# Rotary page columns: one wide transpose and one block-diagonal product for four pages

## The chip, the cores and the metric

One Trainium2 chip, one of its cores. The metric is the device time of one execution in microseconds (us); the number given for a kernel is the median of its timed runs.

## The reference, cut to what matters

One inference step of a hybrid decoder layer, for 1,024 prompt tokens and 64 sample tokens (8 requests of 8 tokens) with the same weights: a combined projection, a pooling mixer, latent attention with 8 heads, a gated merge, and a retrieval of experts. The change lies in the attention of the sample tokens over the paged cache, 32 pages of 128 positions for each request:

```python
def mla_keys(c, kr, p):
    k_nope = jnp.einsum('btc,chd->bthd', c, p['w_uk'])
    kr_b = jnp.broadcast_to(kr[:, :, None, :], k_nope.shape[:-1] + (QK_ROPE,))
    return rmsnorm(jnp.concatenate([k_nope, kr_b], axis=-1), p['k_norm_w'])

def page_step(carry, phys):
    m, l, acc = carry
    c_pg = ckv_pages[phys]
    k_pg = mla_keys(c_pg, kr_pages[phys], p)
    s = jnp.einsum('bqhd,bthd->bhqt', q, k_pg).astype(jnp.float32) * SCALE
    return online_update(m, l, acc, s, c_pg), None
```

A page has 256 latent columns (c) and 32 rotary columns (kr) for each of 128 positions. A score is the product of a query with c in latent form, plus the product of its 32 rotary numbers with kr, times one over the key's norm. The expert part (`peer`) gathers, for each token, 128 rows of 4 KB from `peer_u` and 128 from `peer_v`, and dots and weighs them.

## The kernel before, in words

Everything is fp32. **Experts** is the main program. It is cut into slots: for one slot the four compute engines and SyncE do what belongs to one expert column of 128 tokens. GpSimd issues one indirect gather of 128 rows of `peer_u` and, 20 slots later in the numbering, one of `peer_v` (L1550); VectorE makes a dot product of 1,024 columns (L1658) and, spread over 16 slots, the search for the best experts of a later unit (L1417 to L1488) ; TensorE adds the weighted `peer_v` rows in blocks of 8 products, one block for every 4 slots (L1613). Rings of 8 buffers hold the gathered rows. There are 1,088 such columns.

All other work is laid into these slots by hand: `Main.to(slot)` (L180) issues the main program up to a slot and then lets the caller add its own instructions. Instructions of an engine run in the order in which they are written; semaphores join the engines.

**Pages** (L1730) is the sample attention over the cache. It works in 64 groups (8 requests of 8 groups) of 4 pages; the last group of a request has a fifth page, the request's own new tokens. A group takes 6 slots. For page j of a group:

- `transposes` (L1834) turns the page on TensorE into PSUM (`tp`): two transposes of 128x128 for the latent columns (L1840), one of 128x32 for the rotary ones (L1841).
- `copy_page` (L1917) on ScalarE copies them to SBUF into `cTp[j % 2]`: 128x256 (L1922), then 32x128 (L1923), then a drain.
- `keys` (L1843) on TensorE makes the page's keys, two products of 512 columns (L1850), and then the scores, two products of 64 columns over the latent rows (L1858) and one over 32 rotary rows (L1859). It waits for the square of the page before, since all pages use one PSUM bank for keys.
- `square` (L1930) on ScalarE squares the keys out of PSUM, and `key_norm` (L1990) on VectorE sums the squares per head.

TensorE writes the transposes of page j + 1 ahead of the keys of page j (L1903 to L1908). After the last page of a group ScalarE and VectorE make norms, scaled scores and the maximum over the pages (L1936, L1996, L1941, L2010, L2017); TensorE turns the maxima (`maxima`, L1863) in the first slot of the next group, behind the first transposes of that group and ahead of the others; VectorE makes the new maximum, TensorE spreads it (`spread_maxima`, L1868, behind the keys of page 1), VectorE subtracts (L2033), ScalarE takes exponentials (L1945, L1950, in slot 3), and TensorE weighs the pages (`weigh`, L1875, behind the keys of the last page).

SyncE loads the page table, `w_uk` and the queries before the first group (`load_first`, L1780): latent queries `qlat`, and the rotary queries `qrope`, 32 rows by 512 columns for all requests. It then loads pages by groups, three groups of buffers (L1800), and each request's new rows (L1792). GpSimd clears the buffers that need it (`clear`, L1817).

## Time and profile before

| | |
|---|---|
| median of 3 timed runs | 4246.88 us (4240.99 to 4273.01) |
| the profiled execution, its time | 4212.48 us |
| its span, first to last instruction | 4210.3 us |
| TensorE busy | 3178.9 us (76%) |
| VectorE busy | 2688.5 us (64%) |
| GpSimd busy | 2417.2 us (57%) |
| ScalarE busy | 972.6 us (23%) |
| mean granted TensorE clock | 0.852 of full speed |
| moved by DMA | 1387.22 MB, mean 329 GB/s |
| the pages' stretch (L1840 to L1859) | from 1965.5 to 3412.6 us of the span |

The engines appear as PE (TensorE's matmuls), PEld (its weight loads), DVE (VectorE), ACT (ScalarE), POOL (GpSimd) and SP (SyncE). A row of the timeline has the start, the duration, the engine, the line, what is written and read, and how many records were joined; an fp32 product or weight load of the kernel leaves two records. Ends of matmuls are modelled, so the distance from one start to the next says more than the durations. The time outside the span is 2.2 us.

### The profile page before, as it was taken

What the parts mean: (1) busy time and instruction counts of PE and PEld (TensorE: products, weight loads), DVE (VectorE), ACT (ScalarE), POOL (GpSimd) and SP (SyncE); (2) the same over time, 40 slices, a digit from 0 to 9 for tenths busy, and PEclk for the clock granted to TensorE, in tenths of its full rate; (3) what the DMA queues carried; (4) which work ended last, traced back from release to release, by engine and by line L of the source; (5) the groups of instructions that cost most, each with busy time, mean ns of one, the idle gap of its engine ahead of it and who ended that gap; (6) DMA issues with size and microseconds to landing.
All of it is one profiled execution on the core that took longest, in us unless ns stands there. A gap on an engine that the chain in (4) does not pass through costs nothing.

```text
span 4210.3 us, 46249 instructions
## 1 busy us (share of the span) xinstructions
PE 3178.9 (76%) x13875; PEld 1687.6 (40%) x13875; DVE 2688.5 (64%) x6876; ACT 972.6 (23%) x2083; POOL 2417.2 (57%) x2194
## 2 busy tenths in 40 slices
PE   8896867987796889785888888798887866553335
PEld 5665424533342544342444444444444434230001
DVE  2313976665677766665777777787877765566543
ACT  1200222111122210200444334443353311100000
POOL 0000545665675566666666666666656666577766
PEclk9698978998997889897999999998999977666578
DMA  4445887999999899999888999898989899899999
GB/s 120 100 155 180 312 314 283 411 396 384 384 408 319 285 373 411 397 411 374 320 322 318 329 334 323 306 340 317 331 302 329 321 355 414 330 407 375 364 382 346
DMA packets 431352, 1387.22 MB, mean 329 GB/s; under 512 B 59033, under 2 KB 117370, under 8 KB 426818
## 3 DMA queue, kind: packets, MB, share of 16 engines
q0 software_dynamic: 313344, 1140.99, 71.6%
q1 hardware_dynamic: 117762, 243.29, 16.6%
q8 instruction: 113, 1.85, 0.2%
q14 instruction: 133, 1.09, 0.1%
HBM read 1353.98 MB, written 30.11 MB: 329 GB/s over the span
## 4 chain that ended last, share of the span: by engine, by line
PE 41%; POOL 14%; DVE 12%; DMA 12%; issue 11%; another core or an unknown queue 3%; ACT 2%; DVEq 2%; SPq 1%; ACTq 0%; POOLq 0%
POOL arena L1550 14%; PE ps L1850 10%; PE ps L1613 7%; DMA arena<-in_peer_v,arena 6%; DVE arena L1658 4%; PE ps L915 3%; PE ps L972 2%; PE ps L705 2%; PE ps L1858 2%; DMA arena<-in_peer_u,arena 2%; PE ps L1840 2%; DMA arena<-in_w_peer 2%; PE ps L1859 2%; PE ps L937 2%
## 5 line engine op out<-in xcount | busy, mean ns | idle before, releaser
L1550 POOL DMA_INDIRECT arena<-in_peer_v,arena x1088 | 1185.4, 1090 | 1000.8 <-PE ps L1613 660.5
L1658 DVE CUSTOM_DVE_ANT_0 arena<-arena 128x1024 f32<-128x1024 f32 x1088 | 1321.4, 1222 | 564.2 <-DMA arena<-in_peer_u,arena 457.3
L1550 POOL DMA_INDIRECT arena<-in_peer_u,arena x1088 | 1230.7, 1131 | 766.4 <-DVEq L1488 396.6
L1613 PE MATMUL ps<-arena 128*32 128x512 f32 x4352 | 702.3, 733 | 466.0 <-DMA arena<-in_peer_v,arena 418.7
L1850 PE MATMUL ps<-arena 128*128 128x512 f32 x1056 | 557.5, 653 | 17.8 <-ACT arena L1930 10.1
L1613 PEld LDWEIGHTS ps<-arena 128*32 128x32 f32 x4352 | 146.1, 124 | 865.8 <-issue 852.7
L1990 DVE TENSOR_REDUCE arena<-arena 128x8 f32<-128x512 f32 x264 | 180.7, 685 | 221.1 <-ACT arena L1930 186.2
L972 PE MATMUL ps<-arena 128*128 128x384 f32 (+1 forms) x768 | 249.3, 478 | 57.9 <-DMA arena<-in_w_peer 56.1
L1850 PEld LDWEIGHTS ps<-arena 128*128 128x128 f32 x1056 | 198.7, 209 | 199.8 <-issue 185.3
L1930 ACT ACTIVATE arena<-ps 128x512 f32<-128x512 f32 x264 | 157.7, 597 | 358.2 <-PE ps L1850 291.0
L915 PE MATMUL ps<-arena 128*128 128x384 f32 (+1 forms) x768 | 233.9, 460 | 2.1 <-ACT arena L1129 2.1
L1858 PEld LDWEIGHTS ps<-arena 128*128 128x128 f32 x1056 | 166.7, 199 | 141.0 <-issue 141.0
L972 PEld LDWEIGHTS ps<-arena 128*128 128x128 f32 x768 | 150.3, 202 | 146.2 <-issue 80.1
L1922 ACT ACTIVATE arena<-ps 128x256 f32<-128x256 f32 x264 | 101.4, 384 | 455.0 <-PE ps L1841 261.3
L705 PE MATMUL ps<-arena 128*128 128x384 f32 (+1 forms) x528 | 172.0, 485 | 18.1 <-DVE arena L1201 16.6
L915 PEld LDWEIGHTS ps<-arena 128*128 128x128 f32 x768 | 147.5, 194 | 89.0 <-issue 16.5
L1863 PE MATMUL ps<-const,arena 128*64 128x128 f32 x64 | 22.5, 352 | 173.6 <-DVE arena L2017 97.3
L1858 PE MATMUL ps<-arena 128*128 128x64 f32 x1056 | 151.4, 267 | 0.0
L1627 ACT ACTIVATE arena<-arena 32x1024 f32<-32x1024 f32 x120 | 126.4, 1053 | 90.4 <-DVE arena L1658 69.7
L705 PEld LDWEIGHTS ps<-arena 128*128 128x128 f32 x528 | 102.9, 197 | 88.3 <-issue 28.9
L1840 PE MATMUL ps<-const,arena 128*128 128x128 f32 x528 | 121.7, 315 | 19.8 <-ACTq L1924 13.8
L1875 PE MATMUL ps<-arena 128*64 128x257 f32 x528 | 129.5, 389 | 5.2 <-ACT arena L1950 5.2
(226 smaller groups left out, 4013.0 us busy)
## 6 DMA issues: line engine op xcount, KB each, us to landing
arena<-in_w_merge SPq DMA_DIRECT2D x32, 1536.0 KB
arena<-in_w_peer SPq DMA_DIRECT2D x64, 576.0 KB
arena<-in_cache SPq DMA_DIRECT2D x256, 144.0 KB
arena<-in_peer_u,arena POOLq DMA_INDIRECT x1088
arena<-in_peer_v,arena POOLq DMA_INDIRECT x1088
arena<-in_w_front SPq DMA_DIRECT2D x33, 512.0 KB
arena<-in_w_out SPq DMA_DIRECT2D x24, 512.0 KB
arena<-s_dram SPq DMA_DIRECT2D x68, 128.0 KB
```

The lines of the kernel that those rows point to most:

```text
L705: last = t.matmul(bank, w[:, k, :], xnT[:, k, :], start=k == 0, stop=k == KD - 1)
L915: last = t.matmul(ps[:, 2 + 2 * (d % 2) + a, 0:T], ring[:, a * KD + k, :], xnT[:, k, 0:T], start=k == 0, stop=k == KD - 1)
L972: last = t.matmul(ps[:, 2 + j % 2, 0:T], self.p_ring(j % 3)[:, k, :], xn2T[:, k, :], start=k == 0, stop=k == KD - 1)
L1550: self.nc.gpsimd.indirect_dma_start(out=ring[:, slot, :], out_offset=None, in_=self.I[table], in_offset=bass.IndirectOffsetOnAxis(ap=self. ...
L1613: mm = self.nc.tensor.matmul(self.acc[32 * j:32 * j + 32, n, :], self.diag[:, (q0 + j) // 16 % DIAGS, (q0 + j) % 16, :], self.v_ring[:, (q ...
L1658: self.nc.vector.tensor_tensor_reduce(out=u, in0=u, in1=self.xrep[jg % self.XBUF], scale=1.0, scalar=0.0, op0=ALU.mult, op1=ALU.add, accum ...
L1840: t.transpose(self.tp[:, k * P:(k + 1) * P], src[:, 1 + k * P:1 + (k + 1) * P], self.C["ident"])
L1850: last = t.matmul(self.key, self.cTp[:, j % 2, k * P:(k + 1) * P], self.wuk[:, k, :], start=k == 0, stop=k == 1)
L1858: t.matmul(out, self.cTp[:, j % 2, k * P:(k + 1) * P], self.qlat[:, k, b * NS:b * NS + NS], start=k == 0, stop=False)
L1875: last = self.nc.tensor.matmul(self.acc_ps[0:NS, 0:KL + 1], self.scs[gi % 2][:, j, :], self.source(j, par)[:, 0:KL + 1], start=j == 0, sto ...
L1930: self.nc.scalar.activation(self.sqp[:, j % 2, :], self.key, ACT.Square).then_inc(self.ksq_done, 1)
L1990: self.nc.vector.tensor_reduce(out=self.ssn[:, j, :], in_=self.sqp[:, j % 2, :].rearrange("p (h d) -> p h d", h=H), axis=AX, op=ALU.add).t ...
```

## The change

The rotary columns of four pages are treated together. ScalarE copies the four sets of 32 columns side by side into `ropes` (128x128) during page 0. One transpose of 128x128 in the step of page 1 replaces the four of 128x32, and lands in the same PSUM tile as page 1's latent part, so that page 1's copy is 384 columns wide. The scores' rotary part is one product for the group, behind page 3's latent scores: the stationary side is the turned 128x128, the moving side `qropes`, a block-diagonal 128x256 matrix with the request's 32x64 rotary queries in four blocks and zeros elsewhere. It adds onto the scores of all four pages in PSUM, where only the first product of page 0 now carries the start flag. The fifth page of a request's last group keeps its own small transpose, copy and product. ScalarE's drain behind the copies of pages 1, 2 and 3 is gone. The block-diagonal matrix has two buffers, cleared once by GpSimd; SyncE loads four blocks for each request, one request ahead, from the same DRAM tensor; those of the first request behind GpSimd's clearing. TensorE's block product waits for these loads.

```diff
--- before.py
+++ after.py
@@ -1751,8 +1751,8 @@
         small = take(NS, 8)
         self.m, self.mnew, self.negm, self.corr, self.gmax, self.rl = (small[:, j:j + 1] for j in range(6))
         self.diag, self.acc, self.lat = take(NS, NS), take(NS, KL + 1), take(NS, KL)
-        self.qlat, self.qrope = take(P, 2, H * NS), take(P, H * NS)
-        self.table = take(1, DB * NPAGES).bitcast(I32)
+        self.qlat, self.qropes = take(P, 2, H * NS), [take(P, GP, NS) for _ in range(2)]
+        self.table, self.ropes = take(1, DB * NPAGES).bitcast(I32), take(P, GP * DR)
         self.over = w
         self.latT = take(P, 2, H * NS)
         self.end = w
@@ -1781,15 +1781,22 @@
         sp.dma_start(self.table, self.I["page_table"]).then_inc(self.loaded, 16)
         sp.dma_start(self.wuk, self.I["w_uk"]).then_inc(self.loaded, 16)
         sp.dma_start(self.qlat, self.env["qls_dram"]).then_inc(self.loaded, 16)
-        sp.dma_start(self.qrope[0:DR], self.env["qrs_dram"]).then_inc(self.loaded, 16)
-        sp.wait_ge(self.loaded, 64)
         sp.wait_ge(self.zeroed, 1)
+        self.load_rope(sp, 0, self.loaded)
+        sp.wait_ge(self.loaded, 48 + 16 * GP)
+
+    def load_rope(self, sp, b, done):
+
+        for j in range(GP):
+            sp.dma_start(self.qropes[b % 2][j * DR:(j + 1) * DR, j, :], self.env["qrs_dram"][:, b * NS:(b + 1) * NS]).then_inc(done, 16)
 
     def load_new(self, sp, b):
 
         need(sp, self.pv_done, b * GROUPS)
         rows = self.env["new_rows"]
         sp.dma_start(self.new_page[0:DQ, 1:PGW], rows[b * DQ:b * DQ + DQ, :]).then_inc(self.new_in, 16)
+        if b + 1 < DB:
+            self.load_rope(sp, b + 1, self.new_in)
 
     def load_group(self, sp, gi):
 
@@ -1822,6 +1829,8 @@
         g.memset(self.new_page, 0.0)
         g.drain()
         g.memset(self.new_page[:, 0:1], 1.0)
+        for s in range(2):
+            g.memset(self.qropes[s], 0.0)
         for par in range(3):
             for j in range(GP):
                 g.memset(self.pages[par][:, j, 0:1], 1.0)
@@ -1837,10 +1846,14 @@
 
         need(pe, self.t_out, at + j)
         for k in range(2):
-            t.transpose(self.tp[:, k * P:(k + 1) * P], src[:, 1 + k * P:1 + (k + 1) * P], self.C["ident"])
-        t.transpose(self.tp[0:DR, KL:KL + P], src[:, KL + 1:PGW], self.C["ident"]).then_inc(self.t_done, 1)
-
-    def keys(self, pe, j, at, gi, b):
+            last = t.transpose(self.tp[:, k * P:(k + 1) * P], src[:, 1 + k * P:1 + (k + 1) * P], self.C["ident"])
+        if j == 1:
+            last = t.transpose(self.tp[:, KL:KL + P], self.ropes, self.C["ident"])
+        elif j == GP:
+            last = t.transpose(self.tp[0:DR, KL:KL + P], src[:, KL + 1:PGW], self.C["ident"])
+        last.then_inc(self.t_done, 1)
+
+    def keys(self, pe, j, n, at, gi, b):
 
         t = self.nc.tensor
         pe.wait_ge(self.t_out, at + j + 1)
@@ -1855,8 +1868,14 @@
             need(pe, self.shift_done, gi - 1)
         out = self.small_ps[gi % 2][:, j * NS:(j + 1) * NS]
         for k in range(2):
-            t.matmul(out, self.cTp[:, j % 2, k * P:(k + 1) * P], self.qlat[:, k, b * NS:b * NS + NS], start=k == 0, stop=False)
-        t.matmul(out, self.cTp[0:DR, j % 2, KL:KL + P], self.qrope[0:DR, b * NS:b * NS + NS], start=False, stop=True).then_inc(self.s_done, 1)
+            last = t.matmul(out, self.cTp[:, j % 2, k * P:(k + 1) * P], self.qlat[:, k, b * NS:b * NS + NS], start=j + k == 0, stop=False)
+        if j == GP - 1:
+            if b:
+                pe.wait_ge(self.new_in, 16 * (1 + GP) * b)
+            last = t.matmul(self.small_ps[gi % 2][:, 0:GP * NS], self.cTp[:, 1, KL:KL + P], self.qropes[b % 2].rearrange("p a c -> p (a c)"), start=False, stop=n == GP)
+        elif j == GP:
+            last = t.matmul(out, self.cTp[0:DR, 0, KL:KL + P], self.qropes[b % 2][0:DR, 0, :], start=False, stop=True)
+        last.then_inc(self.s_done, 1)
 
     def maxima(self, pe, gi):
         pe.wait_ge(self.pm_done, gi + 1)
@@ -1879,7 +1898,7 @@
 
         pe.wait_ge(self.page_in[par], (gi // 3 + 1) * 16 * GP)
         if n > GP:
-            pe.wait_ge(self.new_in, b * 16 + 16)
+            pe.wait_ge(self.new_in, 16 * (1 + GP) * min(b + 1, DB - 1) + (16 if b == DB - 1 else 0))
 
     def result(self, pe, b):
 
@@ -1891,7 +1910,7 @@
         last.then_inc(self.latT_done, 1)
 
     def tensor(self, main):
-        main.to(self.first).wait_ge(self.loaded, 64)
+        main.to(self.first).wait_ge(self.loaded, 48 + 16 * GP)
         for gi in range(DB * GROUPS + 1):
             b, g, par, n, at, slot = self.group(gi)
             pe = main.to(slot)
@@ -1905,7 +1924,7 @@
                 if gi < DB * GROUPS and j < n:
                     if j + 1 < n:
                         self.transposes(pe, j + 1, at, par)
-                    self.keys(pe, j, at, gi, b)
+                    self.keys(pe, j, n, at, gi, b)
                 if gi and j == 1:
                     self.spread_maxima(pe, gi - 1)
                 if gi and j == 4:
@@ -1914,14 +1933,20 @@
                 self.result(main.to(slot + 7), b - 1)
 
 
-    def copy_page(self, act, j, at):
+    def copy_page(self, act, j, at, par):
         s = self.nc.scalar
         act.wait_ge(self.t_done, at + j + 1)
 
         need(act, self.s_done, at + j - 1)
-        s.activation(self.cTp[:, j % 2, 0:KL], self.tp[:, 0:KL], ACT.Copy)
-        s.activation(self.cTp[0:DR, j % 2, KL:], self.tp[0:DR, KL:KL + P], ACT.Copy)
-        s.drain().then_inc(self.t_out, 1)
+        wide = KL + P if j == 1 else KL
+        last = s.activation(self.cTp[:, j % 2, 0:wide], self.tp[:, 0:wide], ACT.Copy)
+        if j == 0:
+            s.activation(self.ropes.rearrange("p (a c) -> p a c", a=GP), self.pages[par][:, :, KL + 1:PGW], ACT.Copy)
+            last = s.drain()
+        elif j == GP:
+            s.activation(self.cTp[0:DR, 0, KL:], self.tp[0:DR, KL:KL + P], ACT.Copy)
+            last = s.drain()
+        last.then_inc(self.t_out, 1)
 
     def square(self, act, j, at):
         act.wait_ge(self.key_done, at + j + 1)
@@ -1961,11 +1986,11 @@
             b, g, par, n, at, slot = self.group(gi)
             act = main.to(slot)
             if gi < DB * GROUPS:
-                self.copy_page(act, 0, at)
+                self.copy_page(act, 0, at, par)
             for j in range(5):
                 act = main.to(slot + 1 + j)
                 if gi < DB * GROUPS and j < n and j + 1 < n:
-                    self.copy_page(act, j + 1, at)
+                    self.copy_page(act, j + 1, at, par)
                 if gi and j == 3:
                     self.correct(act, gi - 1)
                     self.exponentials(act, self.group(gi - 1)[3], gi - 1)
```

Line numbers of the changed kernel differ: L1840 becomes L1849, the group's rotary transpose is L1851, L1850 becomes L1863, L1858 becomes L1871, the block product is L1875, L1863 becomes L1882, L1868 becomes L1887 and L1875 becomes L1894.

On TensorE, the middle of a group before, from the transposes of page 2 to the expert block behind page 2's scores; `x2` joins equal rows:

```order
L1840 MATMUL ps<-const,arena 128x128 x2
L1841 MATMUL ps<-const,arena 32x128
L1850 MATMUL ps<-arena 128x512 x2
L1858 MATMUL ps<-arena 128x64 x2
L1859 MATMUL ps<-arena 128x64
L1868 MATMUL ps<-arena,const 128x64
L1840 MATMUL ps<-const,arena 128x128 x2
L1841 MATMUL ps<-const,arena 32x128
L1850 MATMUL ps<-arena 128x512 x2
L1858 MATMUL ps<-arena 128x64 x2
L1859 MATMUL ps<-arena 128x64
L1613 MATMUL ps<-arena 32x512 x8
```

L1840 and L1841 turn a page, L1850 makes keys, L1858 and L1859 scores, L1868 spreads the maxima. The same stretch now:

```order
L1849 MATMUL ps<-const,arena 128x128 x2
L1863 MATMUL ps<-arena 128x512 x2
L1871 MATMUL ps<-arena 128x64 x2
L1887 MATMUL ps<-arena,const 128x64
L1849 MATMUL ps<-const,arena 128x128 x2
L1863 MATMUL ps<-arena 128x512 x2
L1871 MATMUL ps<-arena 128x64 x2
L1613 MATMUL ps<-arena 32x512 x8
```

The rows L1841 and L1859 are gone from between the keys of one page and the next; nothing else moved. The end of the same group on TensorE before, from the scores of page 3 to the keys of the next group's page 0:

```order
L1858 MATMUL ps<-arena 128x64 x2
L1859 MATMUL ps<-arena 128x64
L1875 MATMUL ps<-arena 64x257 x4
L1840 MATMUL ps<-const,arena 128x128 x2
L1841 MATMUL ps<-const,arena 32x128
L1863 MATMUL ps<-const,arena 64x128
L1840 MATMUL ps<-const,arena 128x128 x2
L1841 MATMUL ps<-const,arena 32x128
```

The same place now:

```order
L1871 MATMUL ps<-arena 128x64 x2
L1875 MATMUL ps<-arena 128x256
L1894 MATMUL ps<-arena 64x257 x4
L1849 MATMUL ps<-const,arena 128x128 x2
L1882 MATMUL ps<-const,arena 64x128
L1849 MATMUL ps<-const,arena 128x128 x2
L1851 MATMUL ps<-const,arena 128x128
L1863 MATMUL ps<-arena 128x512 x2
```

The block product (L1875) stands behind page 3's scores, ahead of the weighing (L1894), and the wide transpose (L1851) ahead of page 0's keys, behind the turned maxima (L1882). On ScalarE before, from the first copy of a group to the copies and squares of its page 3:

```order
L1922 ACTIVATE arena<-ps 128x256
L1923 ACTIVATE arena<-ps 32x128
L1922 ACTIVATE arena<-ps 128x256
L1923 ACTIVATE arena<-ps 32x128
L1930 ACTIVATE arena<-ps 128x512
L1922 ACTIVATE arena<-ps 128x256
L1923 ACTIVATE arena<-ps 32x128
L1930 ACTIVATE arena<-ps 128x512
L1922 ACTIVATE arena<-ps 128x256
L1923 ACTIVATE arena<-ps 32x128
L1930 ACTIVATE arena<-ps 128x512
```

The same place on ScalarE now:

```order
L1942 ACTIVATE arena<-ps 128x256
L1944 ACTIVATE arena<-arena 128x128
L1942 ACTIVATE arena<-ps 128x384
L1955 ACTIVATE arena<-ps 128x512
L1942 ACTIVATE arena<-ps 128x256
L1955 ACTIVATE arena<-ps 128x512
L1942 ACTIVATE arena<-ps 128x256
L1955 ACTIVATE arena<-ps 128x512
```

Four copies of 32x128 (L1923 before, one behind each L1922) have become one of 128x128 (L1944) and 128 more columns in the second copy (L1942). On SyncE the first four of the small rotary loads stand behind the wait for GpSimd's clearing and ahead of the first new rows; before, one load of 32x512 stood there and waited for nothing.

## Rows read from the trace of the kernel before

**Rows 1.** Stages: the pages' stretch, and the one behind it.
```profile
core 0: us, PE busy (x) PEld busy (x) DVE busy (x) ACT busy (x) POOL busy (x), PEclk, DMA share, GB/s
...
1965.00:3420.00 1455.00, 1224.81 (x5757) 656.32 (x5753) 1110.51 (x2976) 597.38 (x1319) 931.59 (x805) 0.92 0.89 325
3420.00:3750.00 330.00, 194.21 (x1107) 115.46 (x1107) 188.54 (x493) 31.32 (x67) 211.41 (x190) 0.68 0.97 379
```

**Rows 2.** Groups of instructions from 1965 to 3420 us: busy us, mean ns.
```profile
L1859 PE MATMUL ps<-arena 32*128 32x64 f32 x528 | 115.6, 299 | 0.0
...
L1841 PE MATMUL ps<-const,arena 128*32 128x128 f32 x264 | 77.3, 293 | 0.0
L1923 ACT ACTIVATE arena<-ps 32x128 f32<-32x128 f32 x264 | 66.7, 253 | 0.0
...
L1936 ACT ACTIVATE arena<-arena 128x128 f32<-128x128 f32 x64 | 19.6, 306 | 0.0
```

**Rows 3.** Waits from 1965 to 3420 us: total, times, longest.
```profile
DVE arena L1990 <- ACT arena L1930: 186.2, 131, 5.3
...
PE ps L1863 <- DVE arena L2017: 92.3, 26, 8.0
...
PE ps L1863 <- issue: 75.0, 26, 6.4
...
DVE arena L1990 <- issue: 30.8, 26, 2.9
...
PE ps L1850 <- ACT arena L1930: 10.1, 9, 2.3
```

**Rows 4.** Timeline of TensorE from page 0's scores to page 1's keys.
```profile
2400.38 0.55 PE L1858 MATMUL ps<-arena 128*128 128x64 f32 x4
2400.87 0.43 PE L1859 MATMUL ps<-arena 32*128 32x64 f32 x2
2401.23 0.44 PE L1840 MATMUL ps<-const,arena 128*128 128x128 f32 x2
2401.50 0.27 PE L1841 MATMUL ps<-const,arena 128*32 128x128 f32 x1
2401.61 0.59 PE L1850 MATMUL ps<-arena 128*128 128x512 f32 x1
```

**Rows 5.** Timeline, from page 1's scores to page 2's keys.
```profile
2403.34 0.55 PE L1858 MATMUL ps<-arena 128*128 128x64 f32 x4
...
2404.93 0.59 PE L1850 MATMUL ps<-arena 128*128 128x512 f32 x1
```

**Rows 6.** Timeline, from page 2's scores to page 3's keys, no expert block between.
```profile
2428.41 0.55 PE L1858 MATMUL ps<-arena 128*128 128x64 f32 x4
...
2428.61 0.60 ACT L1930 ACTIVATE arena<-ps 128x512 f32<-128x512 f32 x1 [1.19 <-PE ps L1850]
...
2429.35 0.67 PE L1850 MATMUL ps<-arena 128*128 128x512 f32 x1
```

**Rows 7.** Timeline, an expert block between page 2's scores and page 3's keys.
```profile
2407.49 1.92 PE L1613 MATMUL ps<-arena 128*32 128x512 f32 x16
```

**Rows 8.** Timeline, the end of a group and the beginning of the next.
```profile
2412.01 1.95 PE L1875 MATMUL ps<-arena 128*64 128x257 f32 x8
...
2414.17 0.27 PE L1841 MATMUL ps<-const,arena 128*32 128x128 f32 x1
...
2415.77 0.59 DVE L2017 TENSOR_REDUCE arena<-arena 128x64 f32<-128x256 f32 x1
...
2416.42 0.30 PE L1863 MATMUL ps<-const,arena 128*64 128x128 f32 x1 [1.98 <-issue]
...
2416.88 3.52 PE L1850 MATMUL ps<-arena 128*128 128x512 f32 x4
```

**Rows 9.** Timeline, the beginning of the pages.
```profile
1944.10 16.80 SPq L1800 DMA_DIRECT2D arena<-in_cache  x12
...
1970.53 0.49 DVE L1429 MAX8 arena<-arena 128x8 f32<-128x128 f32 x2 [5.74 <-DMA arena<-s_dram]
```

## The prediction, made before the changed kernel had run

> **What bounds the kernel now.** I read the stages first, then the groups of instructions and the waits inside the pages' stretch, then its timeline. The stages [rows 1] are to show two regimes. Behind the pages the transfers set the pace: their engines are busy 97% of the time at 379 GB/s, and the matmuls are idle four tenths of it. In the pages' stretch (1,455 us, 35% of the span) the transfer engines fall to 89% and 325 GB/s, while TensorE is busy 1,224.8 us, or 84%, and VectorE 1,110.5 us, or 76%. So TensorE sets the pace there, and what it saves moves all later slots forward; the bytes that are left afterwards stay the same, so a gain is kept.
>
> The waits [rows 3] say where TensorE stands still in the stretch: 92.3 + 75.0 us ahead of the turned maxima (L1863), some 2.6 us for each of 64 groups, and only 10.1 us ahead of keys (L1850) for the square of the page before. The first is a chain with a length of its own: page 3's keys, their square, the sums, the root, the scaled scores, the maximum (L2017), the turn. The timeline shows its end [rows 8]: TensorE has weighed and turned page 0 (start 2414.17), and waits until 2416.42 for L2017.
>
> **The length of a page.** A group is then four pages at TensorE's pace plus that chain. What counts is the distance from a page's scores (L1858) to the next page's keys (L1850), start to start. Between pages 0 and 1 it is 2401.61 - 2400.38 = 1.23 us [rows 4]; in it L1859 takes 2401.23 - 2400.87 = 0.36 and L1841 0.11. Between pages 1 and 2, where the spreading of the maxima stands too, it is 1.59 us [rows 5]. Between pages 2 and 3 no transposes stand, only L1859, so 0.84 would be expected; it is 2429.35 - 2428.41 = 0.94 [rows 6]. That is the other limit: the square (L1930) starts 0.20 behind the scores and ends at 2429.21, and the next keys start 0.14 later. Since there is one bank for keys, no distance can be below 0.94 us at full clock. The change shortens distances that are already near it.
>
> **What the change removes, gap by gap.** Counted over the stretch's timeline, 263 distances:
> - 1 to 2: 63 or 64, all at full clock. 1.59 less L1859 and L1841 (0.47) is 1.12, above 0.94. 64 x 0.47 = 30.1 us.
> - 0 to 1 without an expert block, 37 (with those of 2 to 3 in the eight five-page groups): 1.23 - 0.47 = 0.76 would be below the limit, so only 1.23 - 0.94 = 0.29 is gained. 37 x 0.29 = 10.7 us. The square's wait takes back 0.18 of each.
> - 0 to 1 with an expert block between, 36: the block of 1.9 us [rows 7] covers the square, so the whole 0.47 counts, and twice that in the 11 that run at half clock. 25 x 0.47 + 11 x 0.94 = 22.1 us.
> - 2 to 3 with a block, 28: 0.36 each, 10.1 us.
> - 2 to 3 without, 36: at the limit already. Nothing: three quarters of the products go, but these gaps stay at 0.94.
> - The eight fifth pages keep their own transposes and products: 2 us less.
>
> **What it adds on TensorE.** The wide transpose stands where a narrow one stood, ahead of page 0's keys and behind the wait. The two wide ones there start 0.27 apart from L1841 [rows 4], so 0.135 against 0.11: 64 x 0.03 = 1.9 us. The block product of 256 columns has no row before. From below it costs no less than the narrow L1859, 0.36; from above, half of a page's keys, which are four records of 512 columns in 2403.34 - 2401.61 = 1.73 [rows 4, 5], so 0.86. The nearest row is the weighing, 257 columns: eight records in 1.95 us less the tail, 0.24 each [rows 8], so 0.48 to 0.50; I take 0.50. It is 0.14 longer than the product of page 3 that it replaces, but it stands behind page 3's keys, and next on TensorE is the 2.6 us wait, which begins 0.14 later and ends with the chain. Page 0's small transpose, also ahead of that wait, saves nothing for the same reason. Without this cover the product costs 64 x 0.14 = 9 us, at the upper bound 32. Its own wait is for loads issued a request (1455/8 = 182 us) earlier, and nothing is late there.
>
> Sum on TensorE: 30.1 + 10.7 + 22.1 + 10.1 - 2 - 1.9 = 69 us.
>
> **ScalarE and SyncE.** ScalarE loses four copies of 0.253 us [rows 2] and gets one of 128x128 from SBUF, whose like (L1936) takes 0.306, and 128 columns more in one copy; it is busy 41% of the stretch. Page 0's copy is 0.05 longer; the turned maxima behind it wait longer than that, so 0, and 3 us if not. The drains that go have no time of their own in any view: 0 to perhaps 0.1 us for a page, at places where TensorE doesn't wait for copies. The seven later loads of four small blocks queue behind pages that are already there. The first is different: it stands behind GpSimd's clearing, ahead of the page loads that begin at 1944.10, and the scores for VectorE's search come over the same queue behind them; VectorE already waits 5.74 us for them until 1970.53 [rows 9]. The page loads are issued 16.80/12 = 1.40 us apart; four small ones that read no table take at most 5.6, and their landing, which the queue now waits for, stands in no row. The cost lies between 0 (hidden behind the expert block) and twice that, 11; I take 4 us, once, the two more clearings of GpSimd inside it.
>
> **What VectorE lets through.** VectorE works in order, and its 1,110 us must be done in a shorter stretch. It waited for the squares before 131 + 26 of 264 sums [rows 3], 60%; at the others it was itself late, because of a search or a gelu. I moved the arrivals of the squares forward in the row of VectorE, gap by gap, and left its own work as it is: at page 3, where the chain starts, three quarters of TensorE's gain were left. The bounds are 0.6 (only where it waited) and 1. 69 x 0.75 = 52, less 4: 48 us.
>
> The profiled execution took 4212.5 us (span 4210.3 and 2.2 around it), 0.8% below the median of 4246.9. 4212.5 - 48 = 4164.5, a ratio of 0.9886; by the median that is 4198.6. I predict 4199 us, 1.1% faster.
>
> **The granted clock.** The clock of the stretch is 0.92 of full [rows 1]; behind waits the keys run at 1.2 GHz, as in the row of four records in 3.52 us instead of 1.73 [rows 8], and in the thin stretch behind the pages the mean is 0.68. The change takes work out between two waits that keep their length, so TensorE is a little less busy. The Trainium skill, "TensorE: Matmul & The Clock Gate", section "Why this matters for your kernels", asks that TensorE be kept continuously busy and warns of idle gaps, and its Part 4 says that transposes don't count as busy for the gate. By that rule the lost products weigh against the change and the lost transposes don't; the trace agrees so far that low clock follows waits. What it would cost is the last rival.
>
> **Rivals.**
> - VectorE or other parts take more than a quarter: with ScalarE's own batches of work (replicating rows, tables) in the way of earlier squares, a share of 0.4 passes: 28 - 4 = 24 us, 4223. For it: 40% of the sums were late already. Against: the idle time ahead of the other 60%.
> - Transfers bind: 89% busy now, 97% where they bind. By the mean the stretch could shrink by 1455 x (1 - 0.89/0.97) = 120 us, so they don't take the mean gain; but where they bind in parts, half the gain is left, 22 us, 4225.
> - The whole 69 us pass, since the late sums fall where TensorE had an expert block anyway: 65 us, 4181. For it: 2.6 us of wait in each group can also shrink, when VectorE gets its pages earlier.
> - Slower: the clock falls behind every group-end wait. Then page 0 runs at half clock in all 64 groups and not in some 15: (3.52 - 1.73) for the keys and some 0.6 for scores and transposes, 2.4 us a group, 49 x 2.4 = 118 us, 4247 - 48 + 118 = 4317. From 20 more such groups on nothing is gained, from 38 on it is over 1% slower. Against it: the wait gets no longer.
> - The change doesn't do what it says: if the block product had to wait for its loads, each request would stall; the loads are a request ahead, so this has no case of its own.
>
> **How the numbers follow.** Forecast 0.50 (4185 to 4212); the whole gain 0.14; a smaller gain through VectorE 0.21; transfers 0.09; clock 0.06. A measurement of this kernel tells about 1%, 42 us, from no change. Seven tenths of the forecast's case lie beyond that, 0.36, and with the whole gain it is 0.50 faster; 0.44 within 1%; 0.06 slower. The range goes from 4165, the whole 69 us and what the half-clock pages may add, to 4240, where nearly all is taken back.
>
> **What would show it.** Right: distances from scores to keys (L1871 to L1863) of 0.94 in both 0 to 1 and 2 to 3, and 1.12 in 1 to 2; more time waited for the square (10 us before, some 15 now); the block product at 0.5 us; the wait for the turned maxima at 2.4 to 2.9 us a group; the pages' stretch near 1,405 us at 0.90 to 0.93 of the clock; the stretch behind them as long as before. Wrong: the chain from page 3's square to the turned maxima longer by more than 0.3 us on average (VectorE), transfers at 95% and waits for gathers in the stretch, or a clock below 0.88.

## The result, and the profile after

The changed kernel takes 4200.36 us (median of 4 runs, 4181.5 to 4208.6) against 4243.93 us for the kernel before in the same comparison; the ratio is 0.9887, 95% interval 0.9846 to 0.9928. It is 1.1% faster. Run once more, beside other runs of the kernel before, it takes 4196.22 against 4245.77, ratio 0.988 (0.9833 to 0.9927).

The first two profiled executions are a bad measure of that: 4212.48 us before and 4208.6 after. A kernel's executions spread over some 60 us on one chip (before: 4211 to 4276 in 17 runs), so the traces are read here for places and distances, and the times for the whole.

The stages of the changed kernel, columns as in [rows 1]:

```profile
core 0: us, PE busy (x) PEld busy (x) DVE busy (x) ACT busy (x) POOL busy (x), PEclk, DMA share, GB/s
...
1965.00:3410.00 1445.00, 1156.20 (x5198) 583.76 (x5202) 1116.03 (x2985) 578.17 (x1127) 921.75 (x810) 0.90 0.90 330
3410.00:3740.00 330.00, 208.48 (x1106) 122.25 (x1098) 185.49 (x488) 31.22 (x67) 204.69 (x188) 0.67 0.96 377
```

TensorE has lost some 69 us of busy time in the pages' stretch, VectorE's work is as it was, the transfers run at 330 instead of 325 GB/s. Behind the pages the transfers still bind. The pages' stretch starts 4.9 us later than in the trace of before already (GpSimd's clearing at 1935.16 instead of 1930.27), and loses more at its start, as shown below. The fair measure of the pages is from the first turned maxima to the last (start of L1863 before, L1882 after), 63 groups: 1424.6 us before, 1392.2 after.

The distances that the prediction rests on are in TensorE's timeline of the changed kernel (keys are L1863 now, scores L1871, the spreading of maxima L1887, turned maxima L1882, the block product L1875, the weighing L1894):

```profile
1990.84 0.55 PE L1871 MATMUL ps<-arena 128*128 128x64 f32 x4
...
1991.79 1.96 PE L1863 MATMUL ps<-arena 128*128 128x512 f32 x4 [0.17 <-ACT arena L1955]
...
2221.15 0.55 PE L1871 MATMUL ps<-arena 128*128 128x64 f32 x4
...
2222.27 1.88 PE L1863 MATMUL ps<-arena 128*128 128x512 f32 x4
2223.99 0.55 PE L1871 MATMUL ps<-arena 128*128 128x64 f32 x4
2224.48 1.92 PE L1613 MATMUL ps<-arena 128*32 128x512 f32 x16
2226.33 1.99 PE L1863 MATMUL ps<-arena 128*128 128x512 f32 x4
2228.16 0.55 PE L1871 MATMUL ps<-arena 128*128 128x64 f32 x4
2228.54 0.65 PE L1875 MATMUL ps<-arena 128*128 128x256 f32 x2
2229.12 1.95 PE L1894 MATMUL ps<-arena 128*64 128x257 f32 x8
...
2236.82 0.42 PE L1882 MATMUL ps<-const,arena 128*64 128x128 f32 x1 [5.37 <-DVE arena L2042]
...
2237.67 3.62 PE L1863 MATMUL ps<-arena 128*128 128x512 f32 x4
2241.08 0.95 PE L1871 MATMUL ps<-arena 128*128 128x64 f32 x4
...
2248.66 0.55 PE L1871 MATMUL ps<-arena 128*128 128x64 f32 x4
2249.60 0.67 PE L1863 MATMUL ps<-arena 128*128 128x512 f32 x1 [0.39 <-ACT arena L1955]
```

From scores to the next keys: 0.95 with transposes and no expert block (1.23 before [rows 4]), and the row now says what for: the square of the page before (L1955). With the spreading of the maxima 2222.27 - 2221.15 = 1.12 (1.59 before [rows 5]). With an expert block 2226.33 - 2223.99 = 2.34 (2.70 before, by the median). Without transposes and block 0.94, exactly as before [rows 6], but now 0.39 of it is a wait. Over the whole stretch the medians of these kinds are 0.94, 1.12, 2.34 and 0.94; the fifth kind, with transposes and an expert block, fell from 3.08 to 2.68. The block product takes 2229.12 - 2228.54 = 0.58 us.

The waits of the changed kernel, to be set against [rows 3]:

```profile
PE ps L1882 <- DVE arena L2042: 139.0, 39, 8.0
...
DVE arena L2015 <- ACT arena L1955: 135.7, 109, 3.3
...
PE ps L1882 <- issue: 52.7, 15, 11.5
...
DVE arena L2015 <- issue: 36.9, 35, 2.9
...
PE ps L1863 <- ACT arena L1955: 24.5, 32, 7.3
```

Keys wait for the square 32 times instead of 9, 24.5 us instead of 10.1. TensorE's wait ahead of the turned maxima (both rows, "issue" too) has grown from 167.3 to 191.7 us, 3.0 us a group, and VectorE waits for squares 144 times instead of 157: in more pages it is the late one.

### The profile page after: what moved, and what is told of

It reads as the page before. It is cut to its first block, busy times and chain, and to the rows that moved or that the text cites. A ratio compares the mean times of both kernels' runs of the same rounds, so it can differ in the third digit from the quotient of the medians.

```text
span 4206.7 us, 44745 instructions
## 1 busy us (share of the span) xinstructions
PE 3130.8 (74%) x13299; PEld 1620.6 (39%) x13299; DVE 2688.2 (64%) x6876; ACT 954.0 (23%) x1891; POOL 2409.1 (57%) x2196
## 4 chain that ended last, share of the span: by engine, by line
PE 37%; DVE 16%; DMA 13%; POOL 13%; issue 11%; another core or an unknown queue 3%; DVEq 3%; ACT 3%; SPq 1%; ACTq 0%; POOLq 0%
POOL arena L1550 13%; PE ps L1863 8%; DMA arena<-in_peer_v,arena 7%; PE ps L1613 6%; DVE arena L1658 4%; PE ps L705 3%; PE ps L915 2%; PE ps L972 2%; DMA arena<-in_w_peer 2%; PE ps L937 2%; DMA arena<-in_peer_u,arena 2%; PE ps L1894 1%; DVE arena L2015 1%; PE ps L872 1%
## 5 line engine op out<-in xcount | busy, mean ns | idle before, releaser
L1550 POOL DMA_INDIRECT arena<-in_peer_v,arena x1088 | 1202.4, 1105 | 996.6 <-PE ps L1613 659.1
L1550 POOL DMA_INDIRECT arena<-in_peer_u,arena x1088 | 1205.2, 1108 | 774.1 <-DVEq L1488 396.6
L1613 PE MATMUL ps<-arena 128*32 128x512 f32 x4352 | 713.8, 735 | 468.1 <-DMA arena<-in_peer_v,arena 398.6
L1863 PE MATMUL ps<-arena 128*128 128x512 f32 x1056 | 574.2, 670 | 44.5 <-ACT arena L1955 24.5
L1863 PEld LDWEIGHTS ps<-arena 128*128 128x128 f32 x1056 | 200.8, 211 | 233.3 <-issue 224.7
L1955 ACT ACTIVATE arena<-ps 128x512 f32<-128x512 f32 x264 | 158.0, 599 | 406.9 <-PE ps L1863 296.4
L1871 PEld LDWEIGHTS ps<-arena 128*128 128x128 f32 x1056 | 170.1, 202 | 147.6 <-issue 147.6
L1942 ACT ACTIVATE arena<-ps 128x256 f32<-128x256 f32 (+1 forms) x264 | 108.3, 410 | 395.5 <-PE ps L1849 126.3
L1882 PE MATMUL ps<-const,arena 128*64 128x128 f32 x64 | 22.6, 353 | 192.7 <-DVE arena L2042 139.0
L1871 PE MATMUL ps<-arena 128*128 128x64 f32 x1056 | 153.0, 269 | 0.0
L1849 PE MATMUL ps<-const,arena 128*128 128x128 f32 x528 | 119.9, 312 | 36.2 <-issue 16.6
L1894 PE MATMUL ps<-arena 128*64 128x257 f32 x528 | 130.3, 390 | 5.5 <-ACT arena L1975 5.5
```

The source lines that it names most:

```text
L1550: self.nc.gpsimd.indirect_dma_start(out=ring[:, slot, :], out_offset=None, in_=self.I[table], in_offset=bass.IndirectOffsetOnAxis(ap=self. ...
L1613: mm = self.nc.tensor.matmul(self.acc[32 * j:32 * j + 32, n, :], self.diag[:, (q0 + j) // 16 % DIAGS, (q0 + j) % 16, :], self.v_ring[:, (q ...
L1863: last = t.matmul(self.key, self.cTp[:, j % 2, k * P:(k + 1) * P], self.wuk[:, k, :], start=k == 0, stop=k == 1)
L1871: last = t.matmul(out, self.cTp[:, j % 2, k * P:(k + 1) * P], self.qlat[:, k, b * NS:b * NS + NS], start=j + k == 0, stop=False)
L1894: last = self.nc.tensor.matmul(self.acc_ps[0:NS, 0:KL + 1], self.scs[gi % 2][:, j, :], self.source(j, par)[:, 0:KL + 1], start=j == 0, sto ...
L1955: self.nc.scalar.activation(self.sqp[:, j % 2, :], self.key, ACT.Square).then_inc(self.ksq_done, 1)
```

## Experiments

The runs came in three batches, in which the kernel before takes 4245.77, 4218.99 and 4147.47 us. The record names chip 14 for the first batch and chip 2 for the second and the third; why the last two differ is not known. So only kernels of one batch are compared by time. Ratios don't carry over well either: the kernel without the block product has 0.9944 in the second batch and 0.9884 in the third. Distances do. "Stretch" is from the first turned maxima to the last, and "at half clock" is the time in it for which the granted clock was 1.2 GHz.

| kernel | batch | median us | ratio to before, 95% | stretch us |
|---|---|---|---|---|
| changed kernel, again | 1 | 4196.22 | 0.988 (0.9833-0.9927) | 1386.8 |
| before, again (one execution) | 1 | 4248.2 | | 1435.9 |
| changed, late rotary loads | 1 | 4190.36 | 0.9865 (0.9821-0.9909) | 1387.2 |
| before, rotary loads as the change has them | 1 | 4250.85 | 1.0006 (0.9979-1.0034) | 1429.0 |
| changed, late loads, two key banks | 2 | 4178.92 | 0.9893 (0.9858-0.9929) | 1381.6 |
| before, two key banks | 2 | 4217.97 | 0.9998 (0.9981-1.0015) | 1428.3 |
| changed, late loads, narrow transposes back | 2 | 4207.7 | 0.9972 (0.9956-0.9987) | 1410.4 |
| changed, late loads, no block product | 2 | 4198.38 | 0.9944 (0.9922-0.9967) | 1410.8 |
| changed, late loads, again | 3 | 4104.22 | 0.9897 (0.9875-0.9919) | 1354.3 |
| changed, late loads, no block product, again | 3 | 4101.58 | 0.9884 (0.9863-0.9905) | 1349.4 |
| changed, late loads, filled waits | 3 | 4088.89 | 0.9855 (0.9831-0.9879) | 1341.2 |
| changed, late loads, two banks, filled waits | 3 | 4072.91 | 0.9814 (0.9792-0.9836) | 1328.2 |

### Both kernels once more

> The changed kernel once more, unaltered, for a narrower interval and a second trace. The theory of gaps (TensorE's distances from scores to the next keys shorten to 0.94 and 1.12 us, three quarters of it passes VectorE, and something is lost once at the start of the pages) expects a ratio of 0.985 to 0.993, and from the first turned maxima to the last (L1882) 1370 to 1395 us against 1424.6 before. The rival, that most of the measured gain was chance of single runs, expects 0.996 or more and a stretch over 1410 us.

> The kernel before, unaltered, for a second trace: how far two executions of one program differ in the pages' stretch. If the stretch from the first to the last turned maxima (L1863), 1424.6 us in the first trace, lies within 12 us of that, the 32 us between the traces of before and after are the change's; if it varies by 30, nothing can be read from single traces but the distances.

The ratio is 0.988 and the stretch 1386.8 us, as expected by the theory of gaps. The second stretch of before is 1435.9, 11.3 us above the first: near the bound of 12. Two traces of each give 1430 and 1389.5, a gain of 41 us (32 and 49 by pairs).

Behind the last turned maxima the picture is another: 788.7 and 788.3 us before, 797.7 and 799.0 in the changed kernel, 10 us more. With late loads, described below, it is 787.7 in the same batch, so the change need not be the cause; it stays open.

Split at the end of page 3's square, the 63 groups show where it comes from. From the turned maxima to that square: 1017.8 and 1031.8 us before, 973.6 and 961.8 after, 57 less. From the square to the next turned maxima: 406.8 and 404.2 before, 418.6 and 425.0 after, 16 more. The first is TensorE's gain, the second what is given back behind the square. Of these 16 us, 8 lie between the square's end and the start of VectorE's sum (22.9 and 20.1 us before, 28.2 and 30.5 after), and the rest between the sum and the maximum, where VectorE and ScalarE work in turn.

### The start of the pages

In the changed kernel the small rotary loads stand ahead of the page loads. SyncE's rows of the changed kernel at the start of the pages:

```profile
1948.95 1.73 SPq L1791 DMA_DIRECT2D arena<-qrs_dram  x4
1953.09 0.27 SPq L1797 DMA_DIRECT2D arena<-new_rows  x1
1953.41 1.69 SPq L1791 DMA_DIRECT2D arena<-qrs_dram  x4
1956.14 30.47 SPq L1807 DMA_DIRECT2D arena<-in_cache  x12
1986.66 0.43 SPq L1409 DMA_DIRECT2D arena<-s_dram  x1
```

And, from its waits, that of VectorE's search for its scores:

```profile
DVE arena L1429 <- DMA arena<-s_dram: 22.7, 1, 22.7
```

The twelve page loads took 30.47 us to issue instead of 16.80 [rows 9], and the scores that follow them on SyncE came so late that VectorE waited 22.7 instead of 5.7 us. Two kernels tested this from both sides. Late loads in the changed kernel:

```diff
         sp.wait_ge(self.zeroed, 1)
-        self.load_rope(sp, 0, self.loaded)
-        sp.wait_ge(self.loaded, 48 + 16 * GP)
+        sp.wait_ge(self.loaded, 48)
...
-        if b + 1 < DB:
+        if b and b + 1 < DB:
             self.load_rope(sp, b + 1, self.new_in)
...
         for gi in range(3):
             self.load_group(sp, gi)
+        self.load_rope(sp, 0, self.loaded)
...
+            if gi == 1:
+                self.load_rope(sp, 1, self.new_in)
```

> The changed kernel, with the first two sets of small rotary loads moved behind the first page loads; TensorE waits for the first set only at its block product. The theory that these loads and the wait for them put off the page loads and the scores for VectorE's search by 12 us and more (page loads begun at 1956 instead of 1944 us and spread over 30 us instead of 17, VectorE waiting 22.7 us instead of 5.7) expects 10 to 20 us less than the changed kernel, a ratio to before of 0.981 to 0.988, page loads spread over 15 to 20 us, and VectorE's wait under 10 us. The rival, that the start's loss is chance, expects the ratio of the changed kernel and the same spread of the loads.

And the changed kernel's order of loads in the kernel before:

```diff
-        sp.dma_start(self.qrope[0:DR], self.env["qrs_dram"]).then_inc(self.loaded, 16)
-        sp.wait_ge(self.loaded, 64)
         sp.wait_ge(self.zeroed, 1)
+        self.load_rope(sp, 0)
+        sp.wait_ge(self.loaded, 112)
...
         self.load_new(sp, 0)
+        self.load_rope(sp, 4)
...
-        main.to(self.first).wait_ge(self.loaded, 64)
+        main.to(self.first).wait_ge(self.loaded, 176)
```

TensorE waits here for all eight small loads before its first page, where in the changed kernel it waits for four.

> The kernel before, with its one rotary load cut into eight small ones and put where the changed kernel has its own: four behind GpSimd's clearing, with a wait for their landing ahead of the page loads, four behind the new rows. The start theory expects 10 to 20 us more than before, a ratio of 1.002 to 1.005, and in the trace page loads spread over 25 to 30 us and VectorE waiting some 20 us for the search's scores. The rival expects 1.000 and a wait of 6 us.

SyncE's rows in the changed kernel with late loads:

```profile
1973.25 0.30 SPq L1796 DMA_DIRECT2D arena<-new_rows  x1
1974.66 13.61 SPq L1806 DMA_DIRECT2D arena<-in_cache  x12
```

And in the kernel before with the small loads early:

```profile
1960.71 1.73 SPq L1790 DMA_DIRECT2D arena<-qrs_dram  x4
...
1967.91 29.50 SPq L1804 DMA_DIRECT2D arena<-in_cache  x12
1997.45 0.43 SPq L1409 DMA_DIRECT2D arena<-s_dram  x1
```

What holds in every trace is the later first page load. From the page table's load to it, it is 13.9 and 14.9 us in the two traces of before, 21.1 and 20.2 in those of the change, 18.7 in the kernel before with early small loads and 14.7 in the changed one with late loads. The wider spread of the page loads is not certain: 30.47 and 29.50 us with early small loads and 13.61 with late ones, but the second trace of the unaltered changed kernel has its page loads in 12.5 us. VectorE's wait is 22.7, 12.7 and 23.7 us with early loads and 7.0 with late ones.

The price by time is smaller than I expected. The times differ by 5.9 us (4196.2 to 4190.4) and 5.1 us (4245.8 to 4250.9), neither clear of its interval, where 10 to 20 were expected. The traces say more. From the page table's load to the first turned maxima it is 66.8 and 66.6 us before, 81.7 and 78.5 in the changed kernel and 79.6 in the kernel before with early small loads, some 13 us more. But with late loads it is 76.7 us in this batch, and 63.9 to 77.0 in the seven other traces of kernels with late loads. So something else takes 10 us there in some executions, and which part of the 13 us the loads have stays open.

### The floor set by the bank for keys

```diff
-        self.tp, self.key, self.acc_ps = (ps[:, 2 + j, :] for j in range(3))
+        self.tp, self.key, self.acc_ps = ps[:, 2, :], [ps[:, 3, :], ps[:, 7, :]], ps[:, 4, :]
...
-        need(pe, self.ksq_done, at + j)
+        need(pe, self.ksq_done, at + j - 1)
...
-            last = t.matmul(self.key, self.cTp[:, j % 2, k * P:(k + 1) * P], self.wuk[:, k, :], start=k == 0, stop=k == 1)
+            last = t.matmul(self.key[(at + j) % 2], self.cTp[:, j % 2, k * P:(k + 1) * P], self.wuk[:, k, :], start=k == 0, stop=k == 1)
```

ScalarE's square reads the same bank of the two.

> The changed kernel with late rotary loads, and with two PSUM banks for keys in turn, so that keys wait for the square of the page two before. The gap theory, in which the one bank sets a floor of 0.94 us from scores to keys, expects the floor to go: 0.76 us between pages 0 and 1 and 0.48 between pages 2 and 3 where no expert block stands between, some 24 us less on TensorE and 12 to 20 less in all than with late loads alone. The rival, that the 0.94 is a latency of TensorE's own, expects the distances and the time unchanged.

> The kernel before with two banks for keys and nothing else. The gap theory expects little, since only the 36 distances between pages 2 and 3 without an expert block were at the floor, 0.94 to 0.84 us: 4 us on TensorE, a ratio of 0.997 to 1.001. If waits for the square had held the kernel before in another way, it would be 0.99 or less.

Two places of TensorE's timeline with two banks in the changed kernel (keys L1865, scores L1873), pages 2 to 3 and 0 to 1:

```profile
2242.08 0.55 PE L1873 MATMUL ps<-arena 128*128 128x64 f32 x4
2242.47 1.94 PE L1865 MATMUL ps<-arena 128*128 128x512 f32 x4
...
2252.19 0.55 PE L1873 MATMUL ps<-arena 128*128 128x64 f32 x4
2252.58 0.39 PE L1851 MATMUL ps<-const,arena 128*128 128x128 f32 x2
2252.81 1.88 PE L1865 MATMUL ps<-arena 128*128 128x512 f32 x4
```

The floor is gone: 0.39 and 0.62 us, even less than the 0.48 and 0.76 expected, since the scores' four records take 0.39 where the next product has a full 128x128 stationary side, and 0.48 ahead of a smaller one. The 0.94 was the wait for the square and nothing of TensorE's own. In the kernel before, the same edit moves only the one distance at the floor, from 0.94 to 0.84 (median of 36), and the time not at all, ratio 0.9998 (0.9981 to 1.0015), as expected. In the changed kernel the stretch falls from 1387.2 to 1381.6 us only, though 28 distances are 0.55 shorter and 33 some 0.3: the trace has more time at half clock (272 instead of 244 us) and a longer way from the last square to the turned maxima (427.7 instead of 422.6 us). These two traces are from different batches. In its own batch the nearest kernel with one bank is the one without the block product, described below: it has less work for TensorE, and still takes 4198.38 us against 4178.92 with two banks, with intervals of the ratios that hardly meet (0.9922 to 0.9967 and 0.9858 to 0.9929). So the second bank is worth some 20 us by time, as expected.

### Narrow transposes put back

```diff
         if j == 1:
             last = t.transpose(self.tp[:, KL:KL + P], self.ropes, self.C["ident"])
-        elif j == GP:
+        else:
             last = t.transpose(self.tp[0:DR, KL:KL + P], src[:, KL + 1:PGW], self.C["ident"])
```

> The changed kernel with late rotary loads, with three of the four narrow transposes put back on TensorE (pages 0, 2 and 3; nobody reads what they write). The gap theory expects 0.94 us unchanged between pages 0 and 1 without an expert block (0.87 is still below the floor), 1.23 instead of 1.12 between pages 1 and 2, and 0.11 more where an expert block stands: 11 us on TensorE, 5 to 10 us in all. A theory in which each instruction taken from TensorE counts in full expects 1.05 in the first gap and 21 us.

The distances came as the theory of gaps has them: median 0.94 between pages 0 and 1 in spite of the transpose put back, 1.23 with the spreading, 2.72 at least with transposes and a block against 2.61 at least. The stretch did not: 1410.4 us, 23 us more than with late loads in the first batch, where at most 11 were expected. Of these 23, 17 lie directly behind the turned maxima, where page 1's transposes wait for page 0's copies (41.1 us from L1886 to the next transposes in 63 groups, 24.4 in the kernel with late loads), and 8 in keys. Much of this is the batch: the kernel without the block product had 33.9 us at that place in the same batch and 17.0 in the next.

By time there is a fair neighbour in the batch, again the kernel without the block product: 4198.38 us against 4207.7, 9.3 less. The two differ by the three transposes and by the block product, which is worth 2.6 us in the next section, inside the noise. That leaves some 7 us for the transposes, inside the 5 to 10 of the theory of gaps, and speaks against the 21 us of a full count. It is a comparison of neighbours and not of twins.

### The block product's cover

```diff
-            last = t.matmul(self.small_ps[gi % 2][:, 0:GP * NS], self.cTp[:, 1, KL:KL + P], self.qropes[b % 2].rearrange("p a c -> p (a c)"), start=False, stop=n == GP)
```

Each page's scores now begin and end on their own: their first product has the start flag, their second the stop flag, except on a fifth page, whose small rotary product still ends them.

> The changed kernel with late rotary loads, without the block product: the rotary part of the scores of the four pages is left out, its transposes, copies and loads stay. The cover theory (it stands ahead of a wait of 2.6 us for a chain that starts with page 3's keys) expects at most 5 us less. If it is exposed, 0.5 us x 64 = 32 us less.

> The kernel with late rotary loads and without the block product (the rotary part of the four pages' scores left out) once more, beside the one with it. Its first trace had a stretch of 1410.8 us, 308 us of it at half clock, where the one with the product had 1387.2 and 244. The clock theory says that work taken from ahead of the wait for the turned maxima lets the clock fall more often, and expects again 1400 us or more, over 280 us at half clock, and a time not below the one with the product. The rival, chance of one trace, expects 1385 us or less and the same time or up to 5 us less.

In the second batch this kernel, with less work, had a stretch of 1410.8 us and 308 us at half clock, and I took that for the clock theory: work taken from ahead of the wait lets the clock fall. The third batch put it beside its twin. The twin, the changed kernel with late loads once more, was itself expected at 1380 to 1392 us of stretch with some 245 at half clock; it came with 1354.3 and 214, at a ratio of 0.9897 (0.984 to 0.990 expected). So one program's stretch moves by 33 us from batch to batch. First the stretch of the kernel with the product, columns as in [rows 1]:

```profile
1982.80:3337.10 1354.30, 1115.41 (x5101) 568.95 (x5101) 1088.81 (x2912) 572.24 (x1110) 913.76 (x783) 0.92 0.93 340
```

And that of the kernel without it:

```profile
1986.20:3335.60 1349.40, 1084.02 (x4974) 554.82 (x4974) 1087.09 (x2912) 571.88 (x1110) 915.65 (x784) 0.91 0.93 342
```

31 us of busy time less, 4.9 us of stretch less, 2.6 us of time less (4104.2 to 4101.6, inside the intervals). The product, 0.58 x 64 = 37 us of TensorE, is hidden in the wait for the maxima, as predicted. The clock theory foresaw 1400 us or more and over 280 at half clock; it came with 1349.4 and 230, still 16 more at half clock than the twin, but at no cost in time. So the 1410.8 of the second batch was no effect of the product left out.

### Filled waits

```diff
             if gi:
+                for k in range(2):
+                    self.nc.tensor.matmul(self.idle_ps, self.C["ident"], self.wuk[:, k, :], start=True, stop=True)
                 self.maxima(pe, gi - 1)
```

In the kernel with two banks as well, the idle products write into the key bank that comes next, and wait for the square that last read it.

> The changed kernel with late rotary loads and two idle products of 512 columns (1.73 us at full clock, nobody reads them) ahead of the turned maxima in every group, that is inside TensorE's wait. The clock theory expects less time at half clock, under 150 us instead of 245, and 15 to 40 us less in all, since a page's keys at half clock take 1.7 us more. The rival, that the clock costs nothing because those pages have slack, or that the filling delays the turned maxima in the groups without a wait, expects 0 to 15 us more.

> Late rotary loads, two banks for keys and the filling products together, the best version if both theories hold. Two banks alone gave 1381.6 us for the stretch, hardly less than one bank (1387.2), with 272 us at half clock. If the clock had eaten their gain, this one is 10 us or more below the warm one with one bank, with a stretch under 1350 us; if VectorE is what is late, it equals the warm one within 5 us.

The stretch with filling:

```profile
1987.00:3328.20 1341.20, 1194.42 (x5353) 600.30 (x5353) 1088.11 (x2912) 572.12 (x1110) 905.08 (x784) 0.96 0.93 344
```

And with filling and two banks:

```profile
1984.10:3312.30 1328.20, 1184.55 (x5352) 601.25 (x5352) 1087.79 (x2912) 570.29 (x1110) 910.74 (x785) 0.95 0.93 347
```

TensorE's wait for the turned maxima in the kernel with late loads:

```profile
PE ps L1886 <- DVE arena L2046: 187.5, 54, 8.1
```

And in the one with filling:

```profile
PE ps L1887 <- DVE arena L2049: 102.8, 41, 6.4
```

109 us of products that nobody reads (63 x 1.73) make the kernel 15.3 us faster: the granted clock of the stretch rises from 0.92 to 0.96, 117 us at half clock (1.2 GHz) instead of 214. The clock does cost time here, in the first pages behind each wait: from turned maxima to keys the 63 groups take 38.8 instead of 51.8 us, the keys up to their scores 489.4 instead of 507.7. The filling has a price too. From the end of VectorE's maximum to the turned maxima it is 27.3 instead of 3.8 us in all, since in some groups the idle products outlast the wait. With the filling two banks are worth another 16.0 us and 13 us of stretch, no more than the 20 us or so without it, so the clock had not eaten their gain. This version is the fastest of all, ratio 0.9814 (0.9792 to 0.9836).

## Why the prediction was right

Predicted 4199 us, 1.1% faster; measured 4200.36, ratio 0.9887 against 0.9886.

- *TensorE's pace bounds the stretch, and a gain there is kept.* The first half is right: all of the gain that the traces show lies between the first and the last turned maxima. The second isn't confirmed: what follows the pages was to last as long as before, and lasts 10 us longer in both traces of the changed kernel (with late loads it does not).
- *The floor of 0.94 us.* Right, and shown by taking it away. Without it the change would have been counted some 20 us too high on TensorE (37 x 0.18 and 36 x 0.36).
- *The gaps.* Right to 0.01 us in each kind but one: with transposes and an expert block 2.68 came for 2.61. In all the distances from scores to keys fell by 74 us (405.3 and 414.5 before, 340.0 and 331.0 after), where 71 were counted. With the new terms 69 us were summed; only 57 were measured up to page 3's square. Two terms make most of the difference. Page 0's copies, put at 0 "and 3 us if not", do show behind the turned maxima: from L1863 to the next transposes 22.0 and 21.2 us before, from L1882 26.1 and 26.4 after, 4.6 more. And the keys take longer, 506.9 and 512.8 us before, 520.4 and 518.1 after, 9 more. The clock fits this: 226 and 238 us of the stretch were at half clock before, 249 and 254 after, and half of the 19 us added is 9. I had named it as a rival but given it no term in the likeliest case.
- *VectorE lets three quarters through.* 16 of 57 us came back as a longer chain behind page 3's square, 72% passed. The replay of VectorE's row was a good estimate; the simple count of its waits (60%) was too low. The chain is longer by 0.26 us a group, just under the 0.3 that I had named as a sign of being wrong, and the wait for the turned maxima is 3.0 us, just over the 2.4 to 2.9 named. That VectorE is the cause is read from the traces; no run changed VectorE's work.
- *The block product.* 0.58 us, estimated 0.50 (0.36 to 0.86); hidden, as the run without it shows.
- *The start, 4 us once.* The first page load comes 6 us later, and the experiments give 5.9 and 5.1 us by time, neither clear of noise, inside the 0 to 11 given. The traces have 13 us more up to the first turned maxima, outside it. That the page loads can spread over 30 us and hold SyncE was not in the prediction.
- *The sum.* 52 - 4 = 48 were forecast. The timed runs give 43.6 and 49.6. The traces don't add up to that: 41 less in the stretch, 13 more at the start and 10 more behind, 18 in all, and 28 for the whole span, since the two executions of the change also reach the page table's load some 10 us sooner, and nothing of the change stands ahead of it. Two traces of each, from executions that spread over 60 us, can't settle it. So the terms on TensorE are shown, and the agreement of 1.4 us in the time is luck.
- *The rivals.* None of the named ones came alone; the clock's is real in kind, at 9 us and not 118. Its sign, a clock below 0.88, did not come either: 0.91 in the stretch. Transfers: 90% busy, and between the turned maxima no wait for a gather beyond 0.7 us.

## What to carry to other kernels

Before summing what a removed instruction costs, look for the distance at which another engine's answer is awaited: where a single buffer is handed over, part of the gain turns into that wait, and it can be read off from the one place in the old trace where the distance already is that short. An engine that pauses at the end of every round gives free room for work just ahead of the pause, and its clock may be worth more than idle time: filling the pause with idle products brought a third as much as the change itself. The filling must be shorter than the pause, or it delays what the pause waits for. Small loads that something waits for, put ahead of large ones on one queue, put the large ones off, here by 6 us; what that costs in the end has to be measured. And a control run is worth most beside its twin: the stretch of one program moved by 33 us between batches, more than most of the effects sought here.

## What the runs showed of the hardware

- The four records of a pair of 64-column fp32 products take 0.39 us up to a following product with a full 128x128 stationary side, and 0.48 up to one with 32 or 64 of its rows or columns (2242.08 to 2242.47 with two banks, against 2428.41 to 2428.89 in the kernel before). The columns of the following product don't matter: the expert block's 512 columns on a 128x32 side start 0.49 behind the scores, 2223.99 to 2224.48.
- One program took 4245.8 us on chip 14, 4219.0 and then 4147.5 on what the record calls chip 2, 2.4% apart in all, while runs of one batch stay within about 1.5%.
- After a wait of TensorE of 5.4 us a page's keys ran at half speed: 3.41 us from 2237.67 to their scores at 2241.08 in the changed kernel, 1.72 otherwise. Filling that wait with products raised the clock of the whole stretch. The Trainium skill, "TensorE: Matmul & The Clock Gate", section "Why this matters for your kernels", warns of idle gaps between bursts of matmuls, behind which the clock drops. The trace agrees, with 214 us at 1.2 GHz without and 117 us with filling.
